# Gathered rows split by halves of the contraction with a signal each, and the gate arithmetic moved behind the first expert's rows

## The reference, cut to what matters

```python
logits = (x @ router)                                   # 256 x 8
top_val, top_idx = lax.top_k(logits, 2)
top_w = softmax(top_val)
gate = sum(one_hot(top_idx, 8) * top_w[..., None])
for e in range(8):
    y = y + gate[..., e:e+1] * (silu(x @ wg[e]) * (x @ wu[e])) @ wd[e]   # 1024 -> 3584 -> 1024
```

## Time and profile before

| what | value |
|---|---|
| median of three runs | 1395.66 us (1395.16 to 1396.3) |
| profiled execution, its own time | 1395.34 us |
| its span, first to last instruction | 1393.2 us |
| TensorE busy | 1367.8 us (98%) |
| VectorE busy | 1140.5 us (82%) |
| ScalarE busy | 1006.7 us (72%) |
| mean granted TensorE clock | 0.997 of full |

### The profile page before, as it was taken

How to read it: one execution, slowest core, us unless ns; L and a number is a source line. 1 busy time by engine, 2 the same in 40 slices (tenths; PEclk the granted TensorE clock), 3 DMA queues, 4 the chain that set the end, 5 groups by cost and what they waited for, 6 DMA issues and landing times.

```text
span 1393.2 us, 19125 instructions
## 1 busy us (share of the span) xinstructions
PE 1367.8 (98%) x6804; PEld 1138.2 (82%) x6804; DVE 1140.5 (82%) x1197; ACT 1006.7 (72%) x1179; POOL 30.8 (2%) x35
## 2 busy tenths in 40 slices
PE   9999999999999999999999999999999999999996
PEld 7779989988787888888888888888888888888885
DVE  5676655556569999999999999999999989999997
ACT  5665544457548778778877877887787788778775
POOL 1201000000001000000000000000000000000010
PEclk9999999999999999999999999999999999999998
DMA  9457754454479999999999999999999999999960
GB/s 326 168 205 283 281 183 158 134 184 142 161 270 366 393 387 356 395 368 366 382 379 368 365 391 369 366 385 376 374 365 390 368 364 390 373 372 375 383 251 32
DMA packets 180619, 436.93 MB, mean 314 GB/s; under 512 B 4070, under 2 KB 8332, under 8 KB 180572
## 3 DMA queue, kind: packets, MB, share of 16 engines
q1 hardware_dynamic: 176816, 422.74, 82.5%
q0 software_dynamic: 3680, 13.54, 2.7%
q10 hardware_dynamic: 76, 0.02, 0.0%
HBM read 423.18 MB, written 13.11 MB: 313 GB/s over the span
## 4 chain that ended last, share of the span: by engine, by line
PE 91%; DVE 5%; ACT 3%; issue 0%; DMA 0%; DVEq 0%; ACTq 0%
PE ps L1545 26%; PE ps L1546 26%; PE ps L1547 25%; PE ps L1800 3%; PE ps L1802 3%; PE ps L1801 3%; PE ps L2066 2%; DVE w_lo L921 1%; ACT w_hi L530 1%; DVE w_lo L1415 1%; DVE xt_lo L960 0%; PE ps L1572 0%; PE ps L2040 0%; ACT e L585 0%; PE ps L1561 0%
## 5 line engine op out<-in xcount | busy, mean ns | idle before, releaser
L1415 DVE TENSOR_TENSOR w_lo<-ring_a,w_hi 128x1024 fp32r<-128x1024 f32 x384 | 459.9, 1223 | 40.3 <-ACT w_hi L805 30.7
L805 ACT ACTIVATE w_hi<-ring_a 128x1024 fp32r<-128x1024 f32 x384 | 399.7, 1058 | 70.8 <-PE ps L1547 70.8
L1415 DVE TENSOR_TENSOR w_lo<-ring_b,w_hi 128x1024 fp32r<-128x1024 f32 x288 | 345.4, 1223 | 27.5 <-ACT w_hi L805 24.1
L1545 PE MATMUL ps<-w_hi,xg_hi 128*128 128x512 f32 x896 | 356.4, 398 | 2.1 <-DVE w_lo L1415 1.3
L1546 PE MATMUL ps<-w_lo,xg_hi 128*128 128x512 f32 x896 | 353.1, 394 | 0.0
L1547 PE MATMUL ps<-w_hi,xg_lo 128*128 128x512 f32 x896 | 351.5, 392 | 0.0
L805 ACT ACTIVATE w_hi<-ring_b 128x1024 fp32r<-128x1024 f32 x288 | 300.6, 1058 | 54.8 <-PE ps L1547 54.8
L921 DVE TENSOR_TENSOR w_lo<-ring_a,w_hi 128x1024 fp32r<-128x1024 f32 (+2 forms) x119 | 141.7, 1198 | 115.6 <-ACT w_hi L530 115.6
L530 ACT ACTIVATE w_hi<-ring_a 128x1024 fp32r<-128x1024 f32 (+2 forms) x119 | 121.9, 1033 | 129.5 <-PE ps L1802 65.2
L1545 PEld LDWEIGHTS ps<-w_hi,xg_hi 128*128 128x128 f32 x896 | 168.4, 188 | 41.9 <-DVE w_lo L1415 3.7
L1547 PEld LDWEIGHTS ps<-w_hi,xg_lo 128*128 128x128 f32 x896 | 168.3, 188 | 37.8
(11 more groups left out here) (320 smaller groups left out, 1345.9 us busy)
## 6 DMA issues: line engine op xcount, KB each, us to landing
ring_a<-in_moe_wg SPq DMA_DIRECT2D x40, 2048.0 KB, 9.3
ring_a<-in_moe_wu SPq DMA_DIRECT2D x32, 2048.0 KB, 9.5
ring_b<-in_moe_wd SPq DMA_DIRECT2D x32, 2048.0 KB, 9.4
ring_b<-in_moe_wu SPq DMA_DIRECT2D x24, 2048.0 KB, 10.1
ring_a<-in_moe_wd SPq DMA_DIRECT2D x24, 2048.0 KB, 8.5
ring_b<-in_moe_wg SPq DMA_DIRECT2D x16, 2048.0 KB, 10.1
ring_a<-in_ffn_wg SPq DMA_DIRECT2D x5, 2048.0 KB, 8.9
ring_a<-in_ffn_wu SPq DMA_DIRECT2D x5, 2048.0 KB, 7.8
```

What stands on the lines that cost most here:

```text
L805: nc.scalar.activation(w_hi[:, (Q1 + q) % NQ, 0:1024], slot(j % RING2)[:, 1024 * k:1024 * k + 1024], ACT.Copy).then_inc(hi_done, 1)
L1415: v.tensor_tensor(w_lo[:, (Q1 + q) % NQ, 0:1024], slot(j % RING2)[:, 1024 * k:1024 * k + 1024], w_hi[:, (Q1 + q) % NQ, 0:1024].bitcast(F32 ...
L1545: pe.matmul(out_, a_hi, w_hi[:, q, c0:c1], start=first, stop=False)
```

## The change

The gathered rows are handled bank by bank. `gather` signals `gathered` after chunk 3 and after chunk 7, ScalarE's and VectorE's instructions become two of half the size, and TensorE waits for the first half of `xg_lo` ahead of quantum 0 of an item and for the second ahead of quantum 2. `gates()` goes behind quantum 3 of item 0, and the four `keep_pace` matmuls between `gather(0)` and the loop go.

```diff
@@ scalar
             def gathered_heads(n):
-                act.wait_ge(gathered, n + 1)
-                nc.scalar.activation(xg_hi[:, :, :], ps[:, 0:2, :].rearrange("p b (c s) -> p (b c) s", s=P),
-                                     ACT.Copy).then_inc(xg_head, 1)
+                for b in range(2):
+                    act.wait_ge(gathered, 2 * n + b + 1)
+                    nc.scalar.activation(xg_hi[:, 4 * b:4 * b + 4, :], ps[:, b, :].rearrange("p (c s) -> p c s", s=P),
+                                         ACT.Copy).then_inc(xg_head, 1)
@@ vector
-            def gathered_rests(n):
-                dve.wait_ge(xg_head, n + 1)
-                v.tensor_tensor(xg_lo[:, :, :], ps[:, 0:2, :].rearrange("p b (c s) -> p (b c) s", s=P),
-                                xg_hi[:, :, :].bitcast(F32), ALU.subtract).then_inc(xg_rest, 1)
+            def gathered_rests(n, halves=range(2)):
+                for b in halves:
+                    dve.wait_ge(xg_head, 2 * n + b + 1)
+                    v.tensor_tensor(xg_lo[:, 4 * b:4 * b + 4, :], ps[:, b, :].rearrange("p (c s) -> p c s", s=P),
+                                    xg_hi[:, 4 * b:4 * b + 4, :].bitcast(F32), ALU.subtract).then_inc(xg_rest, 1)
...
             choose(0)
-            for q in range(NQ - 1):
+            for q in range(NQ - 2):
                 expert_rest(0, q)
+            gathered_rests(0, (0,))
+            expert_rest(0, NQ - 2)
+            gathered_rests(0, (1,))
+            expert_rest(0, NQ - 1)
             gates()
-            gathered_rests(0)
-            expert_rest(0, NQ - 1)
             extras()
             token_rows()
@@ tensor
-                ins.then_inc(gathered, 1)
+                    if c % 4 == 3:
+                        ins.then_inc(gathered, 1)
...
             def gate_up(i, part, quanta_of, first, f):
                 for kq in quanta_of:
                     q = 4 * first + kq
+                    if f == 0 and part == 0 and kq in (0, 2):
+                        pe.wait_ge(xg_rest, 2 * i + 1 + kq // 2)
                     pe.wait_ge(lo_done, Q1 + QI * i + q + 1)
...
-                pe.wait_ge(xg_head, i + 1)
-                pe.wait_ge(xg_rest, i + 1)
...
             gather(0, False)
-            keep_pace(4, 5, 256)
             with pe.Fori(0, NE - 1) as i:
```

More of the change, by code:

```diff
@@ L408, in load_tokens @@
                 sp.wait_ge(xs_in, 16 * 2 * T)
-                sp.wait_ge(gathered, n)
+                sp.wait_ge(gathered, 2 * n)
                 sp.dma_start(xg_rows[:, :], xs[n]).then_inc(xg_loaded, 16)
@@ L495, in _ @@
             pool.wait_ge(xs_in, 16 * 2 * T)
-            pool.wait_ge(gathered, 1)
+            pool.wait_ge(gathered, 2)
             pool.wait_ge(y_stored, 16 * (NE - 1) + 1)
```

## The result

The changed kernel takes 1398.89 us (median of 10 runs, 1397.85 to 1399.44). The kernel before takes 1395.21 us beside it (10 runs, 1395.06 to 1396.3). The ratio is 1.0024 with a 95% interval from 1.0016 to 1.0033: 3.7 us slower. The prediction said 1399.0 us, most likely slower. The profiled execution of the changed kernel is its fastest, 1397.85 us with a span of 1396.0 us, against 1395.34 us and 1393.2 us before; it has 2.5 to 2.8 us to account for, the median 3.7.

What follows compares the result with a forecast made beforehand. TensorE's matmul stream and its stops were taken as the bound, with VectorE's queue ending the second wait. 1.28 + 2.4 - 0.33 = +3.4 us on 1395.34, plus 0.3 for the median, gave 1399.0 us, range 1396.4 to 1400.1.

Steps and rivals of the forecast that it cites:

- The first wait: TensorE's wait for xg_lo at the start of item 0: its next matmul starts at 411.45, 2.7 us earlier.
- The second wait: TensorE's wait for w_lo of quantum 4, item 0: 1.28 us later, as gates() now stands ahead of it on VectorE.
- The third wait: TensorE's wait for w_lo of quantum 8, item 0: stays at full clock, goes if the clock falls (-0.33 us).
- Hand-overs: Seven hand-overs, each with two half copies and half subtractions: cost taken as 0, 1.1 us with no cover.
- The clock: TensorE's clock falls within the 5.3 us gap before quantum 4; 4.8 us at half rate cost 2.4 us.
- (B): Rival: the clock holds through the gap before quantum 4, leaving only +1.28 us, 1396.9 us; chance 0.13.
- (D): Rival: nothing measurable changes, as gates() finds some cover, 1395.7 us; chance 0.04.
- (C): Rival: TensorE's early start in item 0 is kept, 2.7 us shorter, 1393.0 us; chance 0.03.

Runs made afterwards that it cites:

- The second experiment: Kernel before with only gates() moved behind quantum 3 of item 0, gathered rows in one piece, keep_pace kept: 1398.36 us, ratio 1.0021.
- the first: Changed kernel with gates() put back in front of the first half of the gathered rows: 1396.99 us, ratio 1.0011 to the kernel before.
- the third: Kernel before with the halves alone, gates() ahead of both and the four keep_pace matmuls kept: 1396.23 us, ratio 1.0002.
- the repeated filler run: Changed kernel with a keep_pace filler of eleven between gather and loop, run a second time: 1399.61 us, ratio 1.0028; first time 1399.68 us.
- the filler-of-five experiment: Changed kernel with a keep_pace filler of five between the gather and the loop: 1398.21 us, ratio 1.0019.
- experiment 6, with the halves: Changed kernel with gates() ahead of the first half and w_lo of quantum 4 of item 0 made by GpSimd: 1397.43 us, ratio 1.0013.
- experiment 4: Kernel before without its keep_pace filler matmuls ahead of the expert loop: 1395.69 us, ratio 0.9999.

## Why the prediction was right

**The first wait.** Forecast: `xg_lo` of half 0 ends at 411.17, TensorE starts at 411.45. Measured: it starts at 410.56, 0.08 us late, VectorE's next instruction starts at 411.17, and TensorE at 411.44. Half 1 was in time, with no wait for it.

**The second wait, the cause.** Forecast: `w_lo` of quantum 3 at 413.41, of quantum 4 at 421.1, TensorE at 422.36 with a gap of 5.3 us. Measured: 413.48, 421.18, 422.45 and 5.22, each 0.07 to 0.09 late like the gather of that profile. The second experiment shows that the move of `gates()` alone loses 3.0 of the 3.7 us, the first that undoing it gives back 1.9 us, and the third that the halves alone gain nothing. The parts do not add up to the whole: the fall of the clock is in the second experiment and also in the 1.7 us that the first leaves, as either standstill can bring it. The gain at the front is real and worthless: what TensorE waits for last is VectorE's queue.

**The third wait.** Kept at full clock (the repeated filler run, 0.16 us) and gone with a fall, both as forecast.

**Hand-overs.** No wait of TensorE there, as forecast. The cost of 0 stands: the first and the last transposes of the gathered rows come 2.2 and 2.4 us later than before (530.0 to 532.2, and 1253.1 to 1255.5), so seven hand-overs together add at most 0.2.

**The clock.** The fall came. Its size was wrong in two ways, both too high. Behind the resumption the profile has 2.87 us at 1.2 GHz where 4.8 was taken, and the matmul pitch there is 0.427 against 0.231 us, so each microsecond costs 0.46 and not 0.5: 1.32 us against 2.4. The median leaves more, 3.68 - 1.28 + 0.33 - 0.45 = 2.3 us, near the 2.4 of the forecast. But the profiled run is the fastest of ten, and what the slower ones have more is not seen: eight have a mean clock of 0.995 against its 0.996, which allows a longer or a second stretch at 1.2 GHz.

**How much of the hit is luck.** The forecast was 1395.66 + 3.35 = 1399.0; measured were 1395.21 + 3.68 = 1398.9. The base, the median of three runs, was 0.45 us above the median of the ten runs beside the changed kernel, and the change was forecast 0.33 us too small. The two nearly cancel. Inside the change the clock's term in the profile is 1.1 us smaller than forecast, the late `y_hi` adds 0.45, and the slower runs add the rest.

**The rivals.** (B), without a fall (1396.9), is near what the filler run showed in its fastest execution, 1397.17. (D), no measurable change, is out: the fastest run after, 1397.85, is above the slowest of the kernel before beside it, 1396.3. (C), a kept early start (1393.0), had no run near it. The changed kernel never had `w_lo` of quantum 4 before 421 us.

**Missed.** The late `y_hi` at the end, 0.45 us. It came at a place where the prediction did not look: behind the loop, on an engine whose program had grown.

**What stays open.** Why executions of one kernel differ by up to 4 us once its standstill is moved or filled; what the slower runs of the changed kernel have in addition, about 1 us in the median; and which ScalarE instruction lengthens the idle time ahead of the table load.

## What to carry to other kernels

An engine's idle time in front of a late input is a place where work is free; before such work is moved "behind" the input, see in the timeline whether the engine has any idle time there. Making the first of two waits shorter is worth nothing while another engine's queue sets when the second one ends, and it can cost: behind one gap of 5.2 us the clock fell, where it had held over waits of 0.84 and 1.11 us. When pieces of a change are tried alone, look at the place of the wait and at the granted clock together, since the second can be as large as the first.

## What the runs showed of the hardware

**The stretch at half clock had one length in five profiles.** From the granted clock of the windows, where a window of 1 us with a mean clock of x holds 2(1 - x) us at 1.2 GHz, it was 3.42 us in the changed kernel, 3.42 in the first, 3.42 in the second and 3.42 in the filler-of-five experiment, and 3.40 in the third. The price depends on how much of it lies inside the standstill: 1.57 us (3.42 x 0.46) when TensorE had already resumed, 1.32 in the changed kernel. At the start of the kernel the pitch was low for 6 us with a printed clock of 1.00, so that stretch was a poor measure for this one.

**Short gaps are not safe, and not always dangerous.** The clock fell with standstills of 5.2, 3.1, 3.0, 2.9 and 1.8 us. It held in profiles with 3.4 us (experiment 6, with the halves) and 2.6 us (experiment 4). In the second and third experiments it fell only 1.2 and 0.9 us after the matmuls had resumed, in the filler-of-five experiment 0.5 us after. The Trainium skill (TensorE: Matmul & The Clock Gate, HAM oscillation) describes the pattern of gaps that put TensorE back to half rate. The five profiles with a fall agree, each with 0.50 behind its gap; the one that held over 3.4 us, with falls behind 1.8 and 2.9 us, shows that the length of the gap alone did not decide it here.

**GpSimd can hold VectorE.** While GpSimd subtracted 128x1024 elements, a pair of products on VectorE with two inputs in SBUF, begun 0.27 us into it, took 2.27 us in place of 0.28; in the kernel with the halves a one-input operation of 16 elements, begun 0.41 us into it, took 2.02 us in place of 0.17. Small reductions that started 0.03 and 0.15 us into it ran at their usual 0.20 to 0.22 us; no run here tells whether because they were that early or because of their kind. The Trainium skill (SBUF — State Buffer, SBUF: two separate sides) says that the two engines share one pair of ports under an exclusive lock, taken by VectorE's operations in a fast mode, and by those with two SBUF inputs against a GpSimd operation that reads SBUF. The held pair agrees, 2.27 us against 0.28; whether the one-input operation ran in a fast mode no row shows.
